# The last stage of a GLA, retention and PEER layer on one core: the lower weights formed by GpSimd, value loads in halves

## The reference, cut to what matters

```python
def block(args):
    xb, eb, gb = args          # tokens, chosen experts (128 a token), their gates
    act = jax.nn.gelu(jnp.einsum('tkd,td->tk', u_tab[eb], xb), approximate=False)
    return jnp.einsum('tk,tkd->td', gb * act, v_tab[eb])
```

## Time and profile before

| what | value |
|---|---|
| median of 3 runs | 1941.58 us |
| the profiled execution's own time | 1941.25 us |
| its span, first to last instruction | 1939.4 us |
| mean granted TensorE clock | 0.996 |
| last stage, first to last matmul (L1809) | 1339.8 to 1924.3 us |

### The profile page before, as it was taken

One profiled execution on the slowest core, in us unless ns is written; L12 is line 12 of the kernel. 1 busy time (PEld: TensorE's weight loads), 2 busy tenths in 40 slices (PEclk: granted clock), 3 DMA queues, 4 the chain that ended last, 5 costly groups with the idle time before them and its releaser, 6 DMA issues.

```text
span 1939.4 us, 34300 instructions
## 1 busy us (share of the span) xinstructions
PE 1909.3 (98%) x10830; PEld 1666.6 (86%) x10830; DVE 1348.5 (70%) x2305; ACT 986.0 (51%) x1518; POOL 1402.8 (72%) x962
## 2 busy tenths in 40 slices
PE   9999999999999999999999999999999999999996
PEld 8999888888998888888888888888888888788885
DVE  1844012214688877755899999997888888788887
ACT  5544434436445556567455454545555554455553
POOL 6877878887879889888788777876465565466531
PEclk9999999999999999999999999999999999999998
DMA  8555657577869787777877777777899999999983
GB/s 301 173 152 164 206 152 226 177 234 178 211 150 207 184 188 183 168 186 189 247 168 177 173 172 172 173 172 243 288 336 330 333 327 346 384 328 329 327 315 122
DMA packets 179352, 440.59 MB, mean 227 GB/s; under 512 B 27392, under 2 KB 38528, under 8 KB 162000
## 3 DMA queue, kind: packets, MB, share of 16 engines
q1 hardware_dynamic: 163856, 384.52, 68.7%
q0 software_dynamic: 14416, 50.61, 7.6%
q10 hardware_dynamic: 1008, 4.52, 0.7%
HBM read 426.79 MB, written 12.78 MB: 227 GB/s over the span
## 4 chain that ended last, share of the span: by engine, by line
PE 79%; POOL 6%; issue 5%; DMA 5%; DVE 3%; ACT 1%; DVEq 1%; SPq 0%; POOLq 0%; ACTq 0%
PE ps L1809 23%; PE ps L1764 21%; PE ps L1765 10%; PE ps L1504 7%; PE ps L1506 7%; PE ps L1505 7%; POOL w_lo L1390 4%; DMA v_raw<-in_peer_v 4%; PE ps L1746 3%; POOL u_lo L1428 2%; DVE v_lo L1283 1%; DMA u_raw<-in_peer_u 1%; PE ps L1620 1%; ACT v_hi L734 0%; DMA raw<-in_w_in 0%
## 5 line engine op out<-in xcount | busy, mean ns | idle before, releaser
L1428 POOL TENSOR_TENSOR u_lo<-u_t,u_hi 128x512 fp32r<-128x512 f32 x512 | 653.7, 1301 | 130.4 <-ACT u_hi L641 127.3
L1764 PE MATMUL ps<-xT,u_hi 128*128 128x512 f32 x2048 | 727.1, 399 | 0.4 <-POOL u_lo L1428 0.4
L1765 PE MATMUL ps<-xT,u_lo 128*128 128x256 f32 x2048 | 573.1, 280 | 0.0
L1390 POOL TENSOR_TENSOR w_lo<-raw,w_hi 128x1024 fp32r<-128x1024 f32 x174 | 431.2, 2490 | 99.2 <-ACT w_hi L510 92.8
L641 ACT ACTIVATE u_hi<-u_t 128x512 fp32r<-128x512 f32 x512 | 321.1, 632 | 352.6 <-DVE u_t L1056 351.9
L1764 PEld LDWEIGHTS ps<-xT,u_hi 128*128 128x128 f32 x2048 | 384.6, 188 | 90.4 <-issue 0.7
L1056 DVE STREAM_TRANSPOSE u_t<-u_raw 128x512 f32<-128x512 f32 x512 | 355.1, 701 | 100.7 <-PE ps L1765 59.3
L1765 PEld LDWEIGHTS ps<-xT,u_lo 128*128 128x128 f32 x2048 | 386.6, 189 | 0.0
L510 ACT ACTIVATE w_hi<-raw 128x1024 fp32r<-128x1024 f32 x175 | 184.9, 1059 | 273.7 <-PE ps L1506 264.8
L1453 POOL DMA_INDIRECT sp_rows<-in_peer_v,sp_at x128 | 155.9, 1218 | 195.0 <-DVE far_sum L1267 170.6
L1809 PE MATMUL ps<-v_hi,m_hi 128*128 128x512 f32 x868 | 267.9, 378 | 7.9 <-DVE m_lo L1279 7.1
(11 more groups left out here) (233 smaller groups left out, 2690.7 us busy)
## 6 DMA issues: line engine op xcount, KB each, us to landing
u_raw<-in_peer_u SPq DMA_DIRECT2D x512, 256.0 KB, 4.8
v_raw<-in_peer_v SPq DMA_DIRECT2D x126, 1024.0 KB
raw<-in_w_in SPq DMA_DIRECT2D x111, 512.0 KB, 3.8
raw<-in_w_out SPq DMA_DIRECT2D x32, 512.0 KB, 4.0
raw<-in_w_peer_q SPq DMA_DIRECT2D x128, 128.0 KB, 4.4
act_dram<-act_w ACTq DMA_DIRECT2D x4, 1024.0 KB, 6.8
act_dram<-far_act SPq DMA_DIRECT2D x64, 64.0 KB, 5.1
x_again<-in_x SPq DMA_DIRECT2D x1, 2048.0 KB, 8.0
```

Source lines behind the costliest of these rows:

```text
L1390: pool.tensor_tensor(w_lo[:, k, :], raw[:, k, :], w_hi[:, k % HI_RING, :].bitcast(F32), ALU.subtract).then_inc(lo_done, 1)
L1428: pool.tensor_tensor(u_lo[:, r, :], u_t[:, r, :], u_hi[:, r, :].bitcast(F32), ALU.subtract).then_inc(ulo_done, 1)
L1764: pe.matmul(acc, u_hi[:, r, c], xT[:, :, kt, :], start=kt == 0, stop=False)
L1765: ins = pe.matmul(acc[:, 0:T], u_lo[:, r, c], xT_hi[:, kt, :], start=False, stop=kt == KT - 1)
```

## The change

- GpSimd forms `m_lo` for tiles 4 to 123, in its own order of work, after the five row gathers and the nine gathers of weights with which it begins. TensorE waits for it (`mlo_done`) ahead of each tile of the loop. VectorE forms `m_lo` for tiles 0 to 3 and the last four as before.
- Gathers are placed by tile: behind `m_low(i)` stand those whose slot was freed by a `row_add` placed in a tile before `i` (`add_tile`). In eight tiles that is one pair (row gather and weight gather) a tile, and two pairs in one of them.
- `row_add` waits for the last one's semaphore in place of the `drain`; the drain stays at the first pick behind each `weights`.
- `load_v` is two DMAs of 512 KB, each issued when its own half of tile `i-4` is free. `v_in` counts 32 a tile, so ScalarE still waits for both halves.
- The ten pieces come once in four tiles (from tile 68 to 107), `v_late_raw` first.

```diff
-            def load_v(i, s):
-                sp.dma_start(v_raw[:, 2 * s:2 * s + 2, :].rearrange("p a b -> p (a b)"), v_rows[bass.ds(i, 1)].rearrange("i j d -> j (i d)")).then_inc(v_in[s], 16)
+            def load_v(i, s, freed=None):
+                for h in range(2):
+                    if freed is not None:
+                        sp.wait_ge(v_free, freed + 2 * s + h + 1)
+                    sp.dma_start(v_raw[:, 2 * s + h, :], v_rows[bass.ds(i, 1), :, half_row(h)].rearrange("i j d -> j (i d)")).then_inc(v_in[s], 16)
...
-            for ii in range(P // 8 + 1, P // 8 + 4):
+            for ii in range(P // 8 + 1, P // 8 + 11):
                 for s in range(4):
-                    sp.wait_ge(v_free, ii * 8 + 2 * s + 2)
-                    load_v(ii * 4 + s, s)
-                    beside((ii - P // 8 - 1) * 4 + s)
+                    load_v(ii * 4 + s, s, ii * 8)
+                beside(ii - P // 8 - 1)
...
             def v_high(ii, s, half):
-                act.wait_ge(v_in[s], ii * 16 + 16)
+                act.wait_ge(v_in[s], ii * 32 + 32)
...
             def row_add(n, j):
                 c, k = j % S_SLOTS, n * S_PAIR + j
-                dve.drain()
+                if j in (0, S_CHUNK[0]):
+                    dve.drain()
+                dve.wait_ge(row_added, k + 1)
...
             def v_low(ii, s, half, added=()):
                 dve.wait_ge(v_hi_done, ii * 8 + 2 * s + 1)
-                dve.tensor_tensor(v_lo[:, 2 * s, :], v_raw[:, 2 * s, :], v_hi[:, 2 * (s % 2), :].bitcast(F32), ALU.subtract)
+                ins = dve.tensor_tensor(v_lo[:, 2 * s, :], v_raw[:, 2 * s, :], v_hi[:, 2 * (s % 2), :].bitcast(F32), ALU.subtract)
+                if isinstance(ii, int) and ii == 0:
+                    dve.wait_ge(m_hi_done, s + 1)
+                    m_low(m_lo[:, s % 2, :], m_hi[:, s % 2, :], s, 0, v_lo_done)
+                else:
+                    ins.then_inc(v_lo_done, 1)
                 for n, j in added:
                     row_add(n, j)
-                dve.wait_ge(m_hi_done, ii * 4 + s + 1)
-                m_low(m_lo[:, s % 2, :], m_hi[:, s % 2, :], ii * 4 + s, half, v_lo_done)
...
-            for k in range(S_SLOTS, P):
-                row_gather(k)
-                if k - S_SLOTS + S_PAIR < P:
-                    act_gather(k - S_SLOTS + S_PAIR)
+            def add_tile(k):
+                n, j = divmod(k, S_PAIR)
+                h = j // S_CHUNK[0]
+                return 4 * (S_FIRST + 2 * n + h) + (j - h * S_CHUNK[0]) * 4 // S_CHUNK[h]
+            def m_low(i):
+                pool.wait_ge(m_hi_done, i + 1)
+                pool.tensor_tensor(by_four(m_lo[:, i % 2, :]), tile_w(i // (P // 2), i % (P // 2)), by_four(m_hi[:, i % 2, :].bitcast(F32)), ALU.subtract).then_inc(mlo_done, 1)
+            k = S_SLOTS
+            for i in range(4, P - 4):
+                m_low(i)
+                while k < P and add_tile(k - S_SLOTS) < i:
+                    row_gather(k)
+                    if k - S_SLOTS + S_PAIR < P:
+                        act_gather(k - S_SLOTS + S_PAIR)
+                    k += 1
...
             def v_tile(i, s):
+                if not isinstance(i, int):
+                    pe.wait_ge(mlo_done, i - 3)
                 for h in range(2):
```

More of the change, by code:

```diff
@@ L290, in build @@
         last_in, y_done, y_pool, out_done = sem("last_in"), sem("y_done"), sem("y_pool"), sem("out_done")
-        v_late, late_hi, late_lo, bank_read, gain_ps, shift_ps, shift_done, n_done = (sem(n) for n in ("v_late", "late_hi", "late_lo", "bank_read", "gain_ps", "shift_ps", "shift_done", "n_done"))
+        v_late, late_hi, late_lo, mlo_done, bank_read, gain_ps, shift_ps, shift_done, n_done = (sem(n) for n in ("v_late", "late_hi", "late_lo", "mlo_done", "bank_read", "gain_ps", "shift_ps", "shift_done", "n_done"))
         ln_stat, ln_rstd = sem("ln_stat"), sem("ln_rstd")
@@ L441, in _ @@
                 for s in range(4):
-                    sp.wait_ge(v_free, ii * 8 + 2 * s + 2)
-                    load_v(ii * 4 + s, s)
+                    load_v(ii * 4 + s, s, ii * 8)
             def beside(n):
                 if n < 4:
-                    a, c = n // 2, half_row(n % 2)
+                    sp.dma_start(v_late_raw[:, n, :], v_rows[P - 2 + n // 2][:, half_row(n % 2)]).then_inc(v_late, 16)
+                elif n < 8:
+                    a, c = n // 2 - 2, half_row(n % 2)
                     sp.dma_start(h1_again[:, a, c], h1_dram[a * P:(a + 1) * P, c]).then_inc(h1_in, 16)
[L450 to L454, removed]
-            for ii in range(P // 8 + 1, P // 8 + 4):
+                else:
+                    sp.dma_start(ln2b_sb[:, half_row(n - 8)], ln2_b[0:1, half_row(n - 8)].to_broadcast([P, HALF])).then_inc(last_in, 16)
+            for ii in range(P // 8 + 1, P // 8 + 11):
                 for s in range(4):
-                    sp.wait_ge(v_free, ii * 8 + 2 * s + 2)
-                    load_v(ii * 4 + s, s)
-                    beside((ii - P // 8 - 1) * 4 + s)
-            with sp.Fori(P // 8 + 4, P // 4 - 3) as ii:
+                    load_v(ii * 4 + s, s, ii * 8)
+                beside(ii - P // 8 - 1)
+            with sp.Fori(P // 8 + 11, P // 4 - 3) as ii:
                 for s in range(4):
-                    sp.wait_ge(v_free, ii * 8 + 2 * s + 2)
-                    load_v(ii * 4 + s, s)
+                    load_v(ii * 4 + s, s, ii * 8)
             for ii in range(P // 4 - 3, P // 4):
                 for s in range(4 if ii < P // 4 - 1 else 2):
-                    sp.wait_ge(v_free, ii * 8 + 2 * s + 2)
-                    load_v(ii * 4 + s, s)
+                    load_v(ii * 4 + s, s, ii * 8)
                 if ii == LN2_TURN:
@@ L714, in v_first @@
             def v_first(s):
-                act.wait_ge(v_in[s], 16)
+                act.wait_ge(v_in[s], 32)
                 act.wait_ge(uparts_free, UR + 4 * (P - 1) + 2 * s + 1)
@@ L762, in _ @@
             for s in range(2):
-                act.wait_ge(v_in[s], P // 4 * 16)
+                act.wait_ge(v_in[s], P // 4 * 32)
                 act.activation(v_hi_end[:, 2 * s, :], v_raw[:, 2 * s, :], ACT.Copy).then_inc(v_hi_done, 1)
@@ L1301, in _ @@
                 v_low(0, s, 0)
-            dve.memset(far_sum[:], 0.0)
+            dve.memset(far_sum[:], 0.0).then_inc(row_added, 1)
             dve.wait_ge(gate_in, 16)
@@ L1448, in row_gather @@
                 if j >= S_SLOTS:
-                    pool.wait_ge(row_added, k - S_SLOTS + 1)
+                    pool.wait_ge(row_added, k - S_SLOTS + 2)
                 elif n:
-                    pool.wait_ge(row_added, k - S_CHUNK[1] + 1)
+                    pool.wait_ge(row_added, k - S_CHUNK[1] + 2)
                 c = j % S_SLOTS
```

## The result

The changed kernel takes **1989.6 us** (median of four runs, 1984.9 to 1993.0) where the kernel before, run beside it, takes 1942.2: **ratio 1.0258, 95% interval 1.0237 to 1.0279**, slower. The forecast was 1976.6 us, in a range of 1938 to 2014. The profiled execution took 1992.6 us (span 1990.8), against 1941.25 (1939.4) before: 51.4 us more of span.

What follows compares the result with a forecast made beforehand. TensorE, busy 98% of the span, bounds the kernel before; GpSimd was to become the bound. On 1941.25 us, -10.5 + 7.0 + 1.8 + 25 + 12 = +35.3 gives 1976.6 us, range 1938 to 2014.

Steps and rivals of the forecast that it cites:

- Load waits, -10.5: Last stage: halved loads, thinned pieces and `m_lo` and drains off VectorE take away TensorE's waits, -10.5 us, at worst 0.
- single waits: 4.4 us of the 10.5, outside the stretch of the pieces: waits chained from value load through `v_hi`, `v_lo` to TensorE.
- Tile 4 late, +7.0: `m_lo` of tile 4 stands behind nine weight gathers on GpSimd; TensorE starts at 1366.5 in place of 1359.5, +7.0 us.
- Rival 2: Stores of `far_act` land earlier through gaps in halved loads, tile 4 not late, GpSimd keeps up: 1930.8 us; chance 0.04.
- Clock behind it, +1.8: Behind the idle time of 8.2 us before tile 4 the clock halves: +1.8 us, bounds 0 and 3.4.
- GpSimd as the bound, +25: GpSimd needs 37.6 us per eight tiles against 35.8, held up by VectorE at the port: +25 us in 14 turns.
- Clock in half of the turns, +12: TensorE stalls 1 to 2 us a turn; the clock falls in half of 14 turns, 1.8 us each: +12, bounds 0 and 25.
- VectorE under 4.47: VectorE, held up by at most the 0.70 us of `m_lo`, stays under the 4.47 us a tile.
- The Trainium skill's inferred point: A VectorE `tensor_tensor` should not delay GpSimd's descriptor making; gathers would keep 0.97 us, a turn would need 32.2 us.
- the first rival: GpSimd keeps up, with no wait added at the port: 1939.6 us, no change that can be told; chance 0.25.

Runs made afterwards that it cites:

- experiment 5: Changed kernel with VectorE's `v_lo` subtracting a PSUM bank in place of `v_hi` (one SBUF input, not two): 1940.75 us, ratio 1.0016.
- experiment 1: Kernel before with value loads in halves and pieces thinned, nothing else; drains and `m_lo` on VectorE stay: 1936.65 us, ratio 0.9979.
- experiment 6: Kernel before with loads in halves, pieces thinned, VectorE's wait for the gates behind tile 7; drains and `m_lo` on VectorE kept: 1932.19 us, ratio 0.9973.
- experiment 10: Kernel before with pieces thinned and the wait for the gates behind tile 7; whole loads, drains and `m_lo` on VectorE kept: 1935.70 us, ratio 1.0001.
- 12: The kernel of experiment 6 run once more beside more runs of the kernel before: 1933.69 us, ratio 0.9993.
- experiment 4: Changed kernel with at most three gathers between two `m_lo` of GpSimd, in place of up to four: 1972.83 us, ratio 1.0165.
- experiment 2: Kernel before with halved loads, thinned pieces, semaphore for the drain, wait for the gates behind tile 7; `m_lo` on VectorE: 1941.28 us, ratio 1.0011.
- 7: Kernel before with thinned pieces, semaphore for the drain, wait for the gates behind tile 7; whole loads, `m_lo` on VectorE: 1935.77 us, ratio 0.9977.
- experiment 8: Changed kernel with `m_lo` of tiles 4 to 7 on VectorE, gates' wait behind tile 7, at most three gathers between two `m_lo`: 1960.87 us, ratio 1.0111.
- experiment 11: The kernel of experiment 8 with GpSimd's `m_lo` cut to 4 of its 256 columns: 1943.81 us, ratio 1.0038.

## Why the prediction was right, and where it was off

What set the time is the mechanism of the forecast: GpSimd became the bound because of the port. Its sum was 37.6 us by forecast and 37.8 by trace, but that closeness is luck, since the terms were off and their errors cancelled; and the range of 76 us was wide enough for a forecast that came out 13 us low. By its own steps:

- *Load waits, -10.5.* They are gone from TensorE's path in the changed kernel and in experiment 5, where one wait of 0.6 us is left beside tile 4. They were worth some 9.2 us (experiment 1; and experiment 6, whose stage is 8.4 us shorter with 0.8 us more of idle time at tile 4). The 4.4 us that the forecast called single waits outside the stretch of the pieces were not that: the trace before has two waits over 0.3 us there, of 0.80 and 0.73. I put the gain down to halves and thinning alike; experiment 10 shows that thinning does it. All this is held against the one trace of the kernel before; the ratios of experiments 6, 10 and 12 (0.9973, 1.0001, 0.9993) show 5 us at most.
- *Tile 4 late, +7.0.* Measured 9.8 (10.93 against 1.16 us idle). The gathers and the length of `m_lo` were right (0.70 forecast). What failed is the assumption that the stores of `far_act` land when they did: they came 6.2 us later, 3.1 of it the later start of the stage. Rival 2 had them come earlier, on the ground of the gaps that halved loads leave. The runs show the reverse: with halved loads GpSimd waits 7.02 us for the stores and not 4.17, and so it does in all eleven kernels that have them, while thinning alone leaves 4.82 (experiment 10). Rival 2 had the right place and the wrong sign.
- *Clock behind it, +1.8.* 10.2 us at half, but TensorE worked only 2.95 of them: 1.5.
- *GpSimd as the bound, +25.* Measured 13 x 2.55 = 33.2, and one wait of 0.8 us. The first of the 14 turns, which the forecast counted with the rest, had no stall. The sum of work was right within 0.2 us, but its terms were not: I had `m_lo` at 1.2 (0.89), the row gather at 1.37 (1.51), the weight gather unchanged at 1.125 (1.41). The errors cancel. That the weight gather follows 0.3 us behind the row gather was no reason for it to keep its length: it went to 1.409. The 0.5 us a turn beyond the sum are mostly waits of GpSimd for adds (10.8 us in all); once the runs of gathers are shortened (experiment 4) turn and sum are equal.
- *Clock in half of the turns, +12.* Seven falls in 13 stalls, 1.6 us each (turns of 39.9 against 38.3): 11.2, with stalls of 2.4 us where the forecast had 1 to 2.
- *VectorE under 4.47.* It held: the second `v_lo` grew by 0.31 us and `far_sum` by 0.1, and TensorE waited for `v_lo` once in the whole stage, for 0.3 us.
- *The Trainium skill's inferred point* (the page and section named in experiment 5), by which gathers would stay at 0.97 us and the first rival would come true, fails in the change (1.511 and 1.409) and is nearly met in experiment 5 (1.105 and 0.951). The 32.2 us that the prediction sets beside it don't belong to it: they hold the gathers at 1.215 and 1.125. With 0.97 for both, 9 x (0.97 + 0.97 + 0.61) + 5.6 is 28.6 us. Experiment 5 has 31.0.

Together: -9.2 + 9.8 + 1.5 + 33.2 + 0.8 + 11.2 + 3.0 = 50.3 of the 51.4 us. About 1 us I can't place. So the forecast of +35.3 is 16 too low against the profiled execution: 9 in the turns' stalls, 3 by the stores that the halves hold back, 3 by the later start of the stage, 1 by the loads, 1 unplaced, less 1 on the clock. The median of the runs, 3 us under the profiled one, is 13 above the forecast.

*The semaphore for the drain* was counted with the rest at no price of its own. No run has the changed kernel with the drains, so its part there isn't measured. Without `m_lo` on GpSimd it seems to cost: experiment 2 against 6, on halves, 1.0011 [0.9994, 1.0028] to 0.9973 [0.9956, 0.999]. On whole loads (7 against 10) the ratios say the opposite, 0.9977 to 1.0001, while the stages are 580.4 and 577.6 us. With the kernel before itself at medians from 1935.0 to 1942.2, differences of 0.3% between groups of runs don't decide this. It stays open, as does what makes the signals late.

## What to carry to other kernels

Work moved to an idle engine must be priced beside what that engine and its neighbour already do: here some 32 us of GpSimd's work would have fit into 35.7 us, and became 37.8 beside a VectorE that held the shared port 0.8 of the time (the forecast's estimate); with one operand read from PSUM it was 31.0, and the turns no longer stalled. If an engine issues for several consumers in a fixed order, sum its work over the period in which the order repeats, then look at the longest run ahead of an urgent instruction: the first sets the loss, the second the size of each stall, and here with it how often the clock fell (seven times with four gathers together, once with three). To shorten one instruction in such a loop gives back less than its own length: 3.5 us off the eight `m_lo` made the turn 1.5 us shorter, since the gathers grew by 1.8.

## What the runs showed that I had not expected

- Gathers lengthen when the work between them is shortened: 1.409 us for the weight gather with an `m_lo` of 0.892, 1.573 and 1.668 with one of 0.46 and 0.45. A `tensor_tensor` of GpSimd on four columns took 0.45 us on average and 0.20 at the least.
- TensorE's signals reached ScalarE and SyncE 1.5 to 3.9 us late about once a turn in experiments 2 and 7, 1.1 us late in experiment 1, and in time in the others (the kernel before: one of 1.4 us). The cause is open.
- Loads cut in two, with the same bytes, held other stores back: GpSimd's wait for the stores of `far_act` rose from 4.2 to 4.8 us to 6.6 to 8.6 (three and eleven kernels).
- Stalls of 2.3 to 2.5 us did not always lower the clock: seven of 13 did. Stalls of 1.4 to 1.5 us did so in no case (experiments 4 and 8). The length of the stall alone doesn't part them: 1.95 us before tile 4 of experiment 11 was followed by a clock of 0.50, and 2.90 us in experiment 8 was not.
